# Gated linear attention heads: readout copy in slot 22, norm logarithms ahead of the last gate, second decay logits ahead of the scans

## What is computed

```python
def odd_layer(h, s0, has_meta, pre_g, post_g, w_in, wa2, ba, norm_g, w_out):
    z = rms_norm(h, pre_g) @ w_in
    q, k, v, gate, lr = jnp.split(z, ODD_SPLITS, axis=-1)
    g = jax.nn.log_sigmoid((lr @ wa2 + ba).astype(jnp.float32)) / GLA_TAU
    ...   # chunked scan with decay exp(g), 4 heads, state 256 x 512 per head
    o = rms_norm(o.astype(h.dtype), norm_g).reshape(B, T, GLA_VW) * jax.nn.silu(gate)
    h = h + rms_norm(o @ w_out, post_g)
    return h, st
```

## Time and profile before

| | |
|---|---|
| median of 3 runs | 2062.63 us (2061.0 to 2062.9) |
| profiled execution | 2063.2 us, its span 2061.3 us |
| PE busy | 1959.9 us, 95% |
| PE weight load | 1840.8 us, 89% |
| DVE, ACT, POOL busy | 827.3, 644.0, 688.1 us |
| chain that ended last | PE 77%, DVE 10%, issue 6%, ACT 3% |
| mean granted TensorE clock | 0.967 of full speed |

### The profile page before, as it was taken

The page is one execution under the profiler, slowest core; times in us unless marked ns, Lnnn a source line. Parts: engine busy times, 40 slices in busy tenths (PEclk is TensorE's granted clock), DMA queues, the critical chain, the costliest instruction groups (busy, mean ns, idle before and its releaser), DMA issues.

```text
span 2061.3 us, 38375 instructions
## 1 busy us (share of the span) xinstructions
PE 1959.9 (95%) x14973; PEld 1840.8 (89%) x14973; DVE 827.3 (40%) x1478; ACT 644.0 (31%) x1158; POOL 688.1 (33%) x304
## 2 busy tenths in 40 slices
PE   6999999999999998999889999999999999989997
PEld 6998998899889987999779988988998899879996
DVE  5376337625742665100341454054316422650004
ACT  5232223222221233222342343334225332442122
POOL 2333332223323321545213314322341333225451
PEclk9999999999999999999999999998999899979998
DMA  5655245424533443522324352444244424533322
GB/s 167 200 159 153 73 118 159 127 82 136 157 94 95 142 142 98 171 84 83 91 91 124 113 168 79 123 138 150 75 121 154 134 72 138 180 138 103 101 83 83
DMA packets 357436, 252.53 MB, mean 123 GB/s; under 512 B 15136, under 2 KB 324785, under 8 KB 356721
## 3 DMA queue, kind: packets, MB, share of 16 engines
q1 hardware_dynamic: 316364, 186.75, 31.4%
q10 hardware_dynamic: 40900, 63.42, 9.2%
HBM read 213.62 MB, written 36.96 MB: 122 GB/s over the span
## 4 chain that ended last, share of the span: by engine, by line
PE 77%; DVE 10%; issue 6%; ACT 3%; SPq 2%; DMA 1%; POOL 1%; ACTq 0%; DVEq 0%; POOLq 0%
PE proj L990 64%; PE scratch L990 8%; PE score L990 2%; PE scratch L993 2%; DVE kv L1516 1%; DVE xlo L1388 1%; DVE probw L1544 1%; SPq L467 1%; SPq L459 1%; DVE ek L1787 1%; ACT ek L864 1%; POOL wlo L555 1%; DVE mix L1700 0%; DVE tz L1377 0%; DVE enew L1575 0%
## 5 line engine op out<-in xcount | busy, mean ns | idle before, releaser
L990 PE MATMUL proj<-xhi,wlo 128*128 128x268 f32 x4096 | 1198.0, 292 | 14.7 <-POOL wlo L555 6.3
L990 PE MATMUL proj<-xlo,whi 128*128 128x268 f32 x4096 | 1187.2, 290 | 0.0
L990 PE MATMUL proj<-xhi,whi 128*128 128x268 f32 x4096 | 1186.7, 290 | 0.0
L555 POOL TENSOR_TENSOR wlo<-wraw,whi 128x1024 fp32r<-128x1024 f32 x258 | 634.5, 2469 | 1133.7 <-ACT whi L621 1133.7
L990 PEld LDWEIGHTS proj<-xhi,wlo 128*128 128x128 f32 x4096 | 787.0, 192 | 32.9 <-issue 22.5
L990 PEld LDWEIGHTS proj<-xlo,whi 128*128 128x128 f32 x4096 | 786.4, 192 | 0.8
L990 PEld LDWEIGHTS proj<-xhi,whi 128*128 128x128 f32 x4096 | 783.7, 191 | 0.0
L621 ACT ACTIVATE whi<-wraw 128x1024 fp32r<-128x1024 f32 x258 | 265.1, 1047 | 383.3 <-PE proj L990 278.7
L1377 DVE TENSOR_TENSOR tz<-proj,rstd 128x536 f32<-128x536 f32 x72 | 51.4, 713 | 294.8 <-PE proj L990 294.4
L1695 DVE TENSOR_SCALAR mix<-proj,cols 128x536 f32 x32 | 24.8, 776 | 340.2 <-ACT te L627 179.5
L730 ACT ACTIVATE probw<-score,small 128x128 f32<-128x128 f32 (+3 forms) x64 | 33.2, 524 | 171.5 <-DVE small L1467 171.5
(11 more groups left out here) (267 smaller groups left out, 1747.6 us busy)
## 6 DMA issues: line engine op xcount, KB each, us to landing
wraw<-in_w_in SPq DMA_DIRECT2D x192, 512.0 KB, 4.0
wraw<-in_w_out SPq DMA_DIRECT2D x64, 512.0 KB, 4.0
kv<-in_cache_k SPq DMA_DIRECT2D x128, 128.0 KB, 2.3
kv<-in_cache_v SPq DMA_DIRECT2D x128, 128.0 KB, 2.3
sst<-in_state_gla ACTq DMA_DIRECT2D x32, 512.0 KB, 5.2
out<-sst ACTq DMA_DIRECT2D x32, 512.0 KB, 3.6
hbuf<-h_residual ACTq DMA_DIRECT2D x2, 4288.0 KB, 14.6
vb<-v_sample_rows ACTq DMA_DIRECT2D x32, 256.0 KB, 5.5
```

Source lines behind the costliest of these rows:

```text
L555: pool.tensor_tensor(wlo[:, slot, :, 0:width], wraw[:, kc, :, 0:width], whi[:, slot, :, 0:width].bitcast(F32), ALU.subtract).then_inc(s_lo, 1)
L990: return pe.matmul(out, lhsT, rhs, start=start, stop=stop, skip_group_check=True)
```

## The change

On ScalarE the logarithms of SS0 and SS1 move ahead of the sigmoid of g3, each with its wait for its job; that of SS2 stays behind. In the last head `x_hi` of tiles 2 to 4 moves behind the two logarithms. On VectorE the copy to `srow` moves from slot 23 to slot 22, behind gate g2 and ahead of the last tile's evacuation; in the last head `x_lo` of tiles 0 and 1 moves behind the copy to `og`, 2 to 4 behind the two additions, and 5 and 6 stay behind `gate(3)`. In slot 2 of every head `decay_logits(1)` comes ahead of `running_sums(0)`. TensorE, GpSimd and SyncE have the same instructions in the same order.

```diff
--- before.py
+++ after.py
@@ -948,18 +948,26 @@
                             last = act.activation((gq, gk)[v // 2][:, v % 2, 0:TP], og[:, v, 0:TP], ACT.Square)
                         last.then_inc(s_gsq, 1)
                 if last_head:
-                    x_hi("out1", 0, 5)
+                    x_hi("out1", 0, 2)
                 act.wait_ge(*free_d.at("head", "SO", s))
                 for v in range(4):
                     last = act.activation((gq, gk)[v // 2][:, v % 2, TP:T], og[:, v, TP:T], ACT.Square)
                 last.then_inc(s_gsq, 1)
+                r = ek[:].rearrange("p j t -> p (j t)")[:, 0:T]
+
+                def norm_log(a):
+                    lo_t, hi_t = SS_COLS[a]
+                    act.wait_ge(*full.at("head", f"SS{a}", s))
+                    act.activation(r[:, lo_t:hi_t], bank_of("head", f"SS{a}")[:, 0:hi_t - lo_t], ACT.Ln, scale=1.0 / GV, bias=eps).then_inc(s_fa, 1)
+
+                norm_log(0)
+                norm_log(1)
+                if last_head:
+                    x_hi("out1", 2, 5)
                 sigmoid("head", "g3", n0 + 11, s)
                 if last_head:
                     x_hi("out1", 5, 7)
-                r = ek[:].rearrange("p j t -> p (j t)")[:, 0:T]
-                for a, (lo_t, hi_t) in enumerate(SS_COLS):
-                    act.wait_ge(*full.at("head", f"SS{a}", s))
-                    act.activation(r[:, lo_t:hi_t], bank_of("head", f"SS{a}")[:, 0:hi_t - lo_t], ACT.Ln, scale=1.0 / GV, bias=eps).then_inc(s_fa, 1)
+                norm_log(2)
                 act.wait_ge(*free_a.at("head", "SS2", s))
                 act.activation(r, r, ACT.Exp, scale=-0.5).then_inc(ro_ready.sem, 1)
 
@@ -1838,8 +1846,8 @@
                             evac(n0 + tile, par, tz[:])
                     if c == 1: decay_logits(0)
                     if c == 2:
+                        decay_logits(1)
                         running_sums(0)
-                        decay_logits(1)
                     if c == 3:
                         running_sums(1)
                         references()
@@ -1868,23 +1876,24 @@
                             distances(k + 2)
                     if 17 <= c < 20: factors(c - 15)
                     if c in (18, 20, 22): gate((c - 18) // 2)
-                    if c == 23:
+                    if c == 22:
                         dve.wait_ge(s_so, 8 * s + 8)
                         dve.tensor_copy(srow, score[:, 0:GV]).then_inc(s_srow, 1)
-                        if last_head:
-                            x_lo("out1", 0, 2)
+                    if c == 23:
                         dve.wait_ge(*full.at("head", "SO", s))
                         dve.wait_ge(*free_a.at("head", "OC4", s))
                         dve.tensor_copy(og[:, :, TP:T], bank_of("head", "SO")[:, 0:4 * NB].rearrange("p (v b) -> p v b", v=4)).then_inc(s_fd, 1)
                 if last_head:
-                    x_lo("out1", 2, 4)
+                    x_lo("out1", 0, 2)
                 dve.wait_ge(s_gsq, 2 * s + 2)
                 dve.tensor_tensor(gq[:, :, TP:T], gq[:, :, TP:T], gk[:, :, TP:T], ALU.add).then_inc(s_gadd2, 1)
                 dve.wait_ge(s_gadd2, 2 * s + 1)
                 dve.tensor_tensor(gq[:, 0, TP:T], gq[:, 0, TP:T], gq[:, 1, TP:T], ALU.add).then_inc(s_gadd2, 1)
+                if last_head:
+                    x_lo("out1", 2, 5)
                 gate(3)
                 if last_head:
-                    x_lo("out1", 4, 7)
+                    x_lo("out1", 5, 7)
                 dve.wait_ge(*ro_ready.at("head", "o", s))
                 r = ek[:].rearrange("p j t -> p (j t)")[:, 0:T]
                 for v in range(4):
```

## The result

| | before | changed |
|---|---|---|
| median | 2062.24 us (2061.0 to 2062.9, 4 runs) | 2045.64 us (2044.2 to 2046.8, 4 runs) |
| ratio, 95% interval | 1 | 0.9917 (0.9905 to 0.9928) |
| profiled execution, its span | 2063.2, 2061.3 us | 2045.5, 2043.6 us |
| mean granted clock | 0.967 | 0.971 |

What follows compares the result with a forecast made beforehand. TensorE, busy 1959.9 of 2061.3 us, bounds the kernel; only its waits and lower clock can save much. 4.15 + 16.8 - 0.5 = 20.4 us off 2063.2, with the median 0.6 lower, gives 2042.2 us; range 2038.5 to 2051.5.

Steps and rivals of the forecast that it cites:

- The three waits read from the trace: TensorE's waits for the decay logits' copy and, at each head's end, for the `srow` copy and a logarithm.
- rival (d): Whole kernel: nothing comes of it, the waits hiding a slower release such as weights not ready; 2062.6 us, chance 0.04.
- the prediction's own sign against itself: Forecast is wrong if a new releaser, weight split or addition, stands before SS2 or the next head's chunks.
- rival (b): Heads' ends stay as long, SS2 waiting for something else, say VectorE's additions; 2053.6 us, chance 0.06.
- Decay logits, 4.15 us: Head 0's start: G10 to VT00 falls from 5.57 to 1.42 us, saving 4.15 us once.
- Ends, 16.8 us: Ends of heads 0 to 2, clock kept: 4.9, 6.5 and 5.4 us saved, 16.8 in all, some 6 the clock's.
- VectorE's additions are ready by 2.4 us: At a head's end the additions are ready 2.4 us behind SO, so SS2 can start at 2.5 us.
- The other milestone of the forecast, v0 at 14.9 us: At each end, 14.9 us from the last tile's end to the next tile's, against 19.8, 21.4 and 20.3 before.
- all ends or all but one: The forecast's case: the clock is kept at all heads' ends or all but one; chance 0.50.
- rival (a): Clock still falls at every head's end, 2050.2 us; at one or two, 2044 to 2048; chance 0.37 with mixed cases.
- The last head, -0.5 us: Last head, bound by VectorE: 0.7 us saved, outweighed by clock losses; 0.5 us lost, between 1.4 saved and 2.2 lost.
- The expected loss from the clock behind the tile: Last head, TensorE likely at half speed: up to 0.6 us for the last k and 1.6 for the next tile.

Runs made afterwards that it cites:

- either experiment: The decay logits' move alone on the kernel before, ratio 0.9987; and the changed kernel with the decay logits' old order, ratio 0.9935.
- all but decay: The changed kernel with the old order, running_sums(0) ahead of decay_logits(1); ratio to before 0.9935, 2047.4 us.

## Why the prediction was right, and where it was not

**Direction, range, mechanism.** The time lay in the range, 3.4 us above the forecast. The three waits read from the trace were the ones that went, and rival (d), that nothing comes of it, is refuted by them. But the prediction's own sign against itself came too: an addition stands before SS2 as a new releaser, as rival (b) had it, though at 1.03 us it took back only part of the gain.

**Decay logits, 4.15 us.** Right: 1.42 us from G10 to VT00, and 4.2 us by the stages of the kernels with the new order (21.7, once 20.7) against the three built with the old one (25.9 to 26.0). This pair of profiled executions shows 2.98: 4.15 less the 1.02 us by which G10 came later behind v0, the clock being lower there in the changed kernel (0.68 against 0.82), and 0.15 behind VT00. The time of the whole showed none of it clearly, in either experiment. That the fall in this stage would stay was right as well (0.76 over it), and that the scans' later place costs nothing (the other tiles took 712.25 us for 712.20).

**Ends, 16.8 us.** 14.1 were measured, and the step that failed is the sentence that VectorE's additions are ready by 2.4 us. I took their duration, 0.17 us, from a place where GpSimd had finished (1241.35 + 2.35 = 1243.70), in the kernel before:

```profile
1241.35 2.35 POOL L555 TENSOR_TENSOR wlo<-wraw,whi 128x1024 fp32r<-128x1024 f32 x1
```

```profile
1244.73 0.17 DVE L1882 TENSOR_TENSOR gq<-gq,gk 128x16 f32<-128x16 f32 x1 [0.57 <-ACT gk L954]
```

The copy's edit makes SO, and all behind it, 1.6 us earlier, while GpSimd's last subtraction keeps its time, so the two meet: the addition took 0.88 us. I had asked of each row how long it takes, but not what ran beside it there. That cost 0.7 us at each end and, with 1.03 us of idling left where I had reckoned 0.3, one fall of the clock, 1.5 us. Holding the subtraction took both back at the ends, 3.6 us in sum; they were then 17.7 us shorter than before, 0.9 more than forecast.

The Trainium skill has this in "SBUF — State Buffer", section "SBUF: two separate sides": VectorE with two SBUF inputs and a GpSimd operation that reads SBUF share a pair of ports as "an exclusive lock, not a bandwidth split", and the one that comes later waits until the other is done. The traces agree: the addition's record ends 0.03 us behind GpSimd's subtraction, it is 0.84 us with the copy alone, and 0.17 when the subtraction is over or held.

The other milestone of the forecast, v0 at 14.9 us, failed at each end and with the subtraction held too (16.25, 16.31, 15.83): it left out that VectorE is still at the norm's products when v0's chunk is done. That cost TensorE nothing.

**The clock at the ends.** One fall in three came. The prediction counts this case twice, in the forecast ("all ends or all but one") and in the mixed cases of rival (a), between 2044 and 2048, where the time lies. The evidence is in the eleven traces together: the clock fell at each of the twelve ends that had 1.6 us of idling before SO or 2.2 before SS2; at four of nine with 1.03 us before SS2; at one of three with 0.19 us and three more thin matmuls; at none of nine with 0.3 us and the one thin SS2. So counting the clock's share was right. How much of it is owed to the idling and how much to the thin matmuls beside it these runs do not separate. The Trainium skill's section that the prediction weighed ("TensorE: Matmul & The Clock Gate", "Loop structure matters more than you think") says that the copy out of PSUM does not break the warmth where the next matmuls follow at once. The prediction left that condition out. Here TensorE waited on the reading of a bank, for 1.3 to 2.2 us, and the clock fell at all twelve ends that had such waits.

**The last head, -0.5 us.** +1.55 was measured. Products at 7.99 us behind the evacuation, where they came at 9.43 (1833.34 - 1823.91), are 1.44 saved, the upper bound and twice what I took. ScalarE in the changed kernel:

```profile
1808.81 0.29 ACT L954 ACTIVATE gq<-og 128x8 f32<-128x8 f32 x2
```

It idles neither here (1.08 us before) nor for SS2 (0.31 before): together 1.39. The copy to `og` is done 1.04 us behind the evacuation (3.79 before), and only two tiles of `x_hi` stand ahead of the squares, not the work that I had reckoned with. Neither the copy nor the logarithms alone gained anything in this head (41.81 and 42.59 us); the order of `x_hi` and `x_lo` was not tried by itself. The expected loss from the clock behind the tile did not come: from the products to the second projection tile it is 32.20 us, and was 32.31. How the clock falls in this stage is luck of up to 1.5 us, since it took 40.19 us twice and 38.75 in "all but decay", with the same waits.

**What the sum lacked.** A term for the thin matmuls at the end of slot 21, whose stage takes 19.8, 21.5 or 23.0 us as the clock falls, in every kernel. In this pair it went against the change with 1.5 us.

## What to carry to other kernels

When a step is moved up, look at what the other engines do at its new time, not only at what its instructions took at the old one: a VectorE addition of 0.17 us, begun beside a GpSimd subtraction, took 0.88 here and ended with it. Two waits close together can be worth more removed together than the sum of each, here 14.1 us against 9.3, where the clock falls as long as either stays. And where whole runs spread by more than the effect, compare stages between fixed milestones: where the clock fell alike, they repeated to 0.2 us or better.

## What was unexpected of the hardware

- At the end of slot 21, where TensorE runs small matmuls, most of 16 columns, almost without idling, the clock fell to half in all 44 stages of the eleven traces, for a shorter or longer while also between executions of one kernel. The stage is 19.8, 21.5 or 23.0 us long for that. No run leaves these matmuls out, so that they are the cause is not shown.
- The time before v0, in code that is the same in all these kernels, moved by 7.5 us between profiled executions (1053.9 to 1061.4). Between these two it is mostly TensorE running slower: it was busy for 999.7 us of the one (mean clock 0.98) and for 1006.4 of the other (0.97), with as many matmuls. What moves its clock there was not looked into.
